# Reordering the second block of a two-block transformer kernel on one core: selection early, attentions mixed with dense products, last lifts by row block

## What is computed

```python
h = rmsnorm(x, norm_mix)
(a_x, a_b, a_c, d_q, d_k, d_v, i_q, i_k, i_w, g_q, g_f, g_i, g_g, m_q, gate_logits) = split_cols(h @ w_in)
y_a = a_b * causal_conv3(a_c * a_x, conv_w)
y_b = dsa_attention(q, k, d_v, iq, ik, iw)      # keys chosen by top-64 of an index score
y_c = hgrn2_chunkwise(hq, hk, hv, log_f)        # then rmsnorm and * silu(g_g)
y_m = softmax(mq @ mk) @ mv                     # 4 heads over 256 memory tokens
merged = sum over n of sigmoid(gate_logits)[n] * (branches[n] @ w_lift[n])
x = x + merged @ w_out
x = x + (silu(gate) * up) @ ffn_w_down          # feed-forward on rmsnorm(x)
```

## Time and profile before

| | us |
|---|---|
| median of 3 runs | 2562.72 (2559.86 to 2564.99) |
| profiled execution | 2557.33 |
| its span, first to last instruction | 2555.6 |
| TensorE matmul busy | 2463.1 (96%) |
| VectorE busy | 1544.4 (60%) |
| ScalarE busy | 1172.0 (46%) |
| GpSimd busy | 101.4 (4%) |
| mean granted TensorE clock | 0.986 |

### The profile page before, as it was taken

How to read it: one execution, slowest core, us unless ns; L and a number is a source line. 1 busy time by engine, 2 the same in 40 slices (tenths; PEclk the granted TensorE clock), 3 DMA queues, 4 the chain that set the end, 5 groups by cost and what they waited for, 6 DMA issues and landing times.

```text
span 2555.6 us, 30973 instructions
## 1 busy us (share of the span) xinstructions
PE 2463.1 (96%) x12352; PEld 2055.9 (80%) x12352; DVE 1544.4 (60%) x2297; ACT 1172.0 (46%) x1621; POOL 101.4 (4%) x132
## 2 busy tenths in 40 slices
PE   7999999999999999999999999998999999998999
PEld 5788888888888778887888888786888887777887
DVE  6855655456546575467655747677555657676544
ACT  4643444444444564436434446344444456344442
POOL 2100000000000010000100000000100000000000
PEclk9999999999999999999999999998999999998999
DMA  7355352342653546533754435342754344343652
GB/s 243 118 202 192 132 198 99 134 163 88 225 198 132 184 146 207 178 147 115 280 197 149 152 128 191 104 165 107 263 198 171 143 164 156 110 159 111 235 180 94
DMA packets 263118, 418.93 MB, mean 164 GB/s; under 512 B 12192, under 2 KB 149408, under 8 KB 262976
## 3 DMA queue, kind: packets, MB, share of 16 engines
q1 hardware_dynamic: 258112, 400.15, 44.4%
q0 software_dynamic: 4864, 16.80, 1.8%
HBM read 415.86 MB, written 1.05 MB: 163 GB/s over the span
## 4 chain that ended last, share of the span: by engine, by line
PE 86%; DVE 9%; ACT 2%; issue 1%; DMA 1%; POOL 1%; SPq 0%; DVEq 0%; ACTq 0%
PE bank_L L1818 36%; PE bank_L L1803 23%; PE bank_S L1987 7%; PE bank_O L1987 7%; PE bank_O L1928 3%; DVE wlo L1148 2%; PE bank_S L1803 1%; PE bank_T L1916 1%; PE bank_T L1970 1%; PE bank_T L1831 1%; PE bank_O L1803 1%; DVE sm L1472 1%; DVE pts L1495 1%; PE bank_S L1889 1%; PE bank_L L1889 1%
## 5 line engine op out<-in xcount | busy, mean ns | idle before, releaser
L1148 DVE TENSOR_TENSOR wlo<-raw,whi 128x2048 fp32r<-128x2048 f32 (+1 forms) x332 | 711.6, 2169 | 293.7 <-ACT whi L897 292.9
L897 ACT ACTIVATE whi<-raw 128x2048 fp32r<-128x2048 f32 (+1 forms) x332 | 592.3, 1817 | 58.2 <-DMA raw<-in_w_in 35.3
L1818 PE MATMUL bank_L<-whi,xt_hi 128*128 128x512 f32 x1376 | 547.5, 398 | 7.7 <-DVE wlo L1148 6.3
L1818 PE MATMUL bank_L<-wlo,xt_hi 128*128 128x512 f32 x1376 | 539.0, 392 | 0.0
L1818 PE MATMUL bank_L<-whi,xt_lo 128*128 128x512 f32 x1376 | 538.3, 391 | 0.0
L1803 PE MATMUL bank_L<-whi,xt_hi 128*128 128x512 f32 (+1 forms) x864 | 338.1, 391 | 5.5 <-DVE wlo L1148 5.5
L1803 PE MATMUL bank_L<-wlo,xt_hi 128*128 128x512 f32 (+1 forms) x864 | 334.8, 387 | 0.0
L1803 PE MATMUL bank_L<-whi,xt_lo 128*128 128x512 f32 (+1 forms) x864 | 334.5, 387 | 0.0
L1040 ACT ACTIVATE tok<-bank_L 128x256 f32<-128x256 f32 x132 | 50.7, 384 | 566.1 <-PE bank_L L1818 566.1
L1818 PEld LDWEIGHTS bank_L<-whi,xt_hi 128*128 128x128 f32 x1376 | 260.3, 189 | 61.2 <-issue 7.1
L1818 PEld LDWEIGHTS bank_L<-wlo,xt_hi 128*128 128x128 f32 x1376 | 259.8, 189 | 55.7
(11 more groups left out here) (285 smaller groups left out, 3280.4 us busy)
## 6 DMA issues: line engine op xcount, KB each, us to landing
raw<-in_w_gate_up SPq DMA_DIRECT2D x176, 512.0 KB, 5.9
raw<-in_w_in SPq DMA_DIRECT2D x72, 1024.0 KB, 6.2
draw<-in_w_down SPq DMA_DIRECT2D x44, 1024.0 KB, 6.3
raw<-in_ffn_w_up SPq DMA_DIRECT2D x88, 512.0 KB, 5.7
raw<-in_b_w_qkv SPq DMA_DIRECT2D x36, 1024.0 KB, 6.9
draw<-in_ffn_w_down SPq DMA_DIRECT2D x22, 1024.0 KB, 6.1
raw<-in_w_lift SPq DMA_DIRECT2D x32, 512.0 KB, 4.5
raw<-in_a_w_qkv SPq DMA_DIRECT2D x12, 1024.0 KB, 8.2
```

The lines of the kernel that those rows point to most:

```text
L897: act.activation(wide(whi, w, nkc, ncols)[:, ks, :], wide(raw, w, nkc, ncols)[:, ks, :], ACT.Copy) \
L1148: dve.tensor_tensor(wide(wlo, w, nkc, ncols)[:, ks, :], wide(raw, w, nkc, ncols)[:, ks, :], wide(whi, w, nkc, ncols)[:, ks, :].bitcast(F32 ...
L1818: mm = pe.matmul(banks[bank][:, :], xx[:, k, t * P:(t + 1) * P], ww[:, k, :], start=(k == 0 and q == 0), stop=(k == KC - 1 and q == 2))
```

## The change

Only the second block's stage list and what serves it are changed.

- `norms` replaces the layer and RMS norms: same arithmetic, row blocks interleaved, one GpSimd round per row block. `rows_of` replaces `split(r)`: row block 0 is turned inside the mem V product (`mid`), row block 1 inside the pair IQ, MQ.
- A stage of kind `fill` is a product that is cut into 16 steps of k (3 matmuls each, 6 of half width if turned) and dealt out over the steps of another stage: gate (3,1) over select, DQ over the memory attention, AC and AB over the DSA attention, gate (2,0) over HGRN (its row block 0 ahead of the states, 1 ahead of the outputs).
- Selection is early. New order: mem K, mem V, IQ and MQ, narrow chunk, gate (3,0), select with gate (3,1), head norm and turn of MQ, memory attention with DQ, lifts 3, gate (1,0), gate (1,1), AX, DSA attention with AC and AB, gate (0,0), conv, lifts 1, GF, GQ, gate (0,1), lifts 0, GI, GG, HGRN with gate (2,0), gate (2,1), lifts 2, w_out. The eight top-k rounds are a stage `topk` in three parts: ahead of gate (1,0), of gate (1,1) and of AX.
- An attention with fill rotates its scores through S0 and S1 alone.
- Conv writes its result in float32 and a stage `conv_end`, behind lifts 1, splits it.
- `lifts`: the last two lifts go row block by row block, with r's row block 0 turned ahead of the last quarter and row block 1 turned inside the first product of w_out.

```diff
+            add("select", iqT=iqT, kkT=kkT, sel=sel, ready=is_turned, fill=[gate_st])
+            q_ok = headnorm(heads_of(tc, 128), 4, 128, gains[:, l, 256:384], is_in[1])
+            turn(tc, q_ok, mqT)
+            add("exp_table")
+            st = linear(lhs, w_cols(C_DQ), NW, "act", dst=tc, after=[])
...
+            o_is = attention(units, 128 ** -0.5, [], (turn_done, n["turn"]), [], fill=[st], ps=ps2)
             ylhs = split(ym, o_is, (yt_hi, yt_lo), nkc=4)
-            lift(3, ylhs, gates(3), first=True)
+            lift(3, ylhs, 0, gate_0, first=True)
+            lift(3, ylhs, 1, gate_1, first=True)
+            add("topk", sel=sel, rounds=(0, 3))
...
+            gate_01 = gate(0, 1, tb)
+            add("decays", l=l, counts=counts)
+            lift(0, ylhs, 0, gate_00)
+            lift(0, ylhs, 1, gate_01)
...
+        def filled(fill, i, steps):
+
+            per, total = T * KC, T * KC * len(fill)
+            a, b = total * i // steps, total * (i + 1) // steps
+            return [(st, max(a - q * per, 0), min(b - q * per, per)) for q, st in enumerate(fill)
+                    if a < (q + 1) * per and b > q * per]
...
+        def split_at(fill, i, steps):
+
+            for q, st in enumerate(fill):
+                for h in range(2):
+                    if i == (2 * q + h) * steps // (2 * len(fill)):
+                        return [st["w"] + 1, (h,)]
+            return None
```

VectorE's part of an attention and of the last lifts, and TensorE's last lines in a step:

```diff
+                    steps = len(U) + 3
+                    for i in range(steps):
                         if i < len(U):
                             maxima(i)
-                        if i >= 2:
+                        if 2 <= i < len(U) + 2:
                             copies(i - 2)
                             reciprocal(i - 2)
+                        if split_at(st["fill"], i, steps):
+                            split_lo(*split_at(st["fill"], i, steps))
...
+                elif st["kind"] == "lifts":
+                    w = st["w"]
+                    split_upto(w + 1)
+                    for half in range(2):
+                        lifted(w + half, 0, half, (SB, OB)[half][0], st["held"][half])
+                    lifted(w, 1, 0, SB[1], st["held"][0])
+                    rows_lo(st["rows"], 0)
+                    lifted(w + 1, 1, 1, OB[1], st["held"][1])
+                    split_upto(w + 2)
...
+                        for late, a, b in filled(st["fill"], i, len(U) + 3):
+                            product(late, a, b)
```

More of the change, by code:

```diff
@@ L250, in renorm @@
             st = add("renorm", norm=norm, dst=dst, alpha=alpha, lhs=lhs, bias=bias, w=n["w"], gbv=n["gb"],
-                     rows=x if norm == "layer" else r)
+                     rows=x if norm == "layer" else r, second=second[0] if lhs else None,
+                     when=[(x_ready, n["xr"] + t + 1) for t in range(T)])
+            second[0] = None
             if lhs:
@@ L594, in lift @@
[L594 to L609, removed]
-            conv_in = (aev, n["aev"])
-            ym = blk(3).rearrange("p (t c) -> p t c", t=T)
+            def gate(branch, half, dst):
+                linear(lhs, w_cols(C_GATE + branch * D + half * NW), NW, "act", dst=dst, func=ACT.Sigmoid,
+                       after=[(dev, n["dev"]), (rope_done, n["rope"])])
+                return (dst, n["aev"])
@@ L686, in build @@
+            headnorm(heads_of(tc, HD), 8, HD, gains[:, l, 0:64], dq_in)
+            q_ok = rope(heads_of(tc, HD), 8, 1, dq_in)
+            turn(tc, q_ok, dqT)
+            add("exp_table")
+            fill = [linear(lhs, w_cols(c0), NW, "act", turned=True, dst=blk(b_).rearrange("p (h s) -> p h s", s=SEQ), after=[])
+                    for b_, c0 in ((1, C_AC), (2, C_AB))]
+            conv_in = (aev, n["aev"])
             units = []
@@ L694, in build @@
                 units.append(dict(rows=rows, dv=HD, sink=None))
-            o_is = attention(units, HD ** -0.5, [(aev, small_ok[1])], (turn_done, n["turn"]), [gate_st], lead=0, in_twos=True)
-            ylhs = split(yb, o_is, (yt_hi, yt_lo), nkc=4)
-            lift(1, ylhs, held_gates)
+            o_is = attention(units, HD ** -0.5, [(aev, small_ok[1])], (turn_done, n["turn"]), [], in_twos=True, fill=fill,
+                             ps=ps2)
+            gate_00 = gate(0, 0, tc)
+            add("conv", l=l, after=conv_in)
@@ L698, in build @@
+            add("lifts", lhs=ylhs, rows=second[0], held=(gate_0, gate_1), w=n["w"])
+            for half in range(2):
+                chunks.append(([(0, cols(w_lift[l, 2], half * NW, (half + 1) * NW))], 4, NW))
+            for t in range(T):
+                for half in range(2):
+                    finishes(n["w"] + half, t, t == T - 1)
+            n["w"] += 2
+            n["dev"] += 4
             load_gains([norm_ffn[l]], [(dev, n["dev"]), (o_done, n["unit"])])
-            lhs = split(r, (dev, n["dev"]), (xt_hi, xt_lo))
@@ L1774, in turn_heads, with product @@
                     held[name] = (turn_done, at["turn"] + t + 1)
[L1776 removed]
+            def product(st, first=0, last=None):
                 at = st["at"]
@@ L2052, in _ @@
                         held[name] = (rel_done, at["rel"] + e + 1)
+                        for late, a, b in filled(st["fill"], e, 4 * T):
+                            product(late, a, b)
                 elif st["kind"] == "hgrn":
```

456 lines of the change are left out of this document (273 added, 183 removed).

## The result

The changed kernel takes **2572.14 us** (median of 7 runs, 2567.3 to 2576.11), the kernel before 2559.86 beside it: ratio 1.0046, 95% interval 1.003 to 1.0062. It is **slower by 12.3 us**, where 20 less was forecast, and lies above the range. A repetition (first experiment) gives 1.0041.

What follows compares the result with a forecast made beforehand. TensorE's dense products were taken to set the pace, with only overhead to win. Terms of -10.9 and -9.4 us in the two layers sum to -20.3: 2542.4 for the median, 2537.0 for the profiled execution; range 2520 to 2566.

Steps and rivals of the forecast that it cites:

- norms: Mem K to third product: rows turned inside products, weight split following them on VectorE; -5.6 / -1.4 us.
- select: Scores interleaved with a gate product: overhead 6.2 us, little dearer than the unstalled second layer; -4.4 / -0.1 us.
- mq behind select: Head norm of mq after select's last accumulation, uncovered: TensorE stands 8.2 us, plus 2 for the clock; +10.2 / +10.2.
- memory attention: Attention over the memory with DQ as fill: 9.1 us of overhead plus 1.2 bare ahead of the lift; -1.2 / -1.2.
- DSA attention: Filled with two turned products: 11.2 us own work plus 4.5 of waits from half-splits of weights; -3.5 / -7.3.
- conv, forget gates: Conv moved under a gate product, its split behind the lifts: new overhead 0 and 0.6 us; -3.8 / -8.8.
- first lifts, branch 0: Decay exponentials delay the second lift's split on ScalarE: wait 3.9 us, GI's split 0.6, clock 1.5; +6.0 / +6.0.
- HGRN: A gate product as fill closes both gaps, leaving 9.0 us; -5.1 / -3.4.
- last lifts, w_out: Lifts by row block, then w_out: TensorE waits 3.8 us for its split, stage 40.3; -4.3 / -4.2.
- Top-k: Eight rounds moved under lifts, gates and AX: 43 us of VectorE work fits 44.3 of products, DQ's turn late; +0.8 / +0.8.
- Rival 4: Slower: lower clock in filled stretches, 192 us in all; slower by over 5 from a 13% share, 2590 at a quarter; chance 0.07.
- Rival 3: DSA attention fill paced by VectorE's and ScalarE's queues, every half-split bare: 33 us instead of 9, 2566; chance 0.12.

Runs made afterwards that it cites:

- e1: Changed kernel with VectorE's head norm of mq issued ahead of select instead of behind it: 2548.79 us, ratio 0.9958.
- e4: Changed kernel with VectorE's head norm and rope of DQ issued ahead of AX instead of behind its split: 2556.24 us, ratio 0.999.
- e7: Changed kernel with mq and DQ norms earlier, w_out's first split between last lifts, decays behind first lifts, third gate's weights split ahead of the logarithms: 2511.31 us.
- e11: e7 with DSA attention half-splits one step later and, second layer, the first lift's split ahead of the second logarithms: 2499.76 us, ratio 0.9784.
- e12: e7 with coarser fill in select (two groups of scores, then 12 matmuls): 2511.5 us.
- e15: e11 with mq's head norm put back behind select: 2522.2 us, ratio 0.9854.
- e8: e7 with select unfilled, gate product (3, 1) as a whole behind the scores: 2517.04 us.
- e14: e11 with the fills of select and of both attentions undone: 2515.17 us, ratio 0.9825.
- e0: The changed kernel repeated unaltered beside the kernel before: 2570.55 us, ratio 1.0041.
- e13: e11 with coarser fill in select (two groups of scores, then 12 matmuls): 2498.41 us, ratio 0.9762, the best version.

## Why the prediction was wrong

Forecast and measured change of each term, first layer / second layer, from the windows above (dense work taken off as the forecast did). The mq row is the wait of 7.8 with the 2.3 and 2.6 that the attention behind it takes over the 20.0 of e1; the memory attention's row is that 20.0 and the 1.1 ahead of its lift:

| term | forecast | measured |
|---|---|---|
| norms | -5.6 / -1.4 | -4.9 / -1.3 |
| select | -4.4 / -0.1 | -2.0 / +2.3 |
| mq behind select | +10.2 / +10.2 | +10.1 / +10.4 |
| memory attention | -1.2 / -1.2 | -1.3 / -1.3 |
| turn of DQ late | +0.8 / +0.8 | +5.3 / +5.2 |
| DSA attention | -3.5 / -7.3 | -1.5 / -6.1 |
| conv, forget gates | -3.8 / -8.8 | -2.6 / -3.1 |
| first lifts, branch 0 | +6.0 / +6.0 | +5.7 / +6.9 |
| HGRN | -5.1 / -3.4 | -4.6 / -2.9 |
| last lifts, w_out | -4.3 / -4.2 | -3.6 / -2.8 |
| sum | -10.9 / -9.4 | +0.6 / +7.3 |

Some 2 us more per layer lie in turns and products outside these windows.

**What held.** The waits that were looked for came as foretold: mq 7.8 (8.2 forecast), lifts 4.0 (3.9), w_out 3.9 (3.8). A bare wait for the first DSA scores came too, at 2.3. All told, the gaps that the forecast named were right to a few tenths. Its sum for the DSA attention's own work comes to 11.0 where it says 11.2, and the queue of *Top-k* to 0.5 where it says 0.8; neither matters.

**The step that failed is *Top-k*:** "VectorE's queue there ... 43 us of work with 1.8 of waits for the first transfer, against 44.3 of products. The turn of DQ is late by 0.8." It summed VectorE's work and one wait. The queue has a second, 3.16 behind ScalarE, and a GpSimd round 1.27 longer than mq's, together 4.4; the turn was late by 5.3 and 5.2. With its clock the late turn is worth 15 us (e4) where 1.6 was forecast: alone enough to turn -20 into about -7 (part of the 15 stands in the table's row for the DSA attention). The rest of the way to +12 is, by the table, in the two steps that follow (6.9 and 4.8 too low in sum), in the DSA attention (3.2), in the last lifts (2.1) and in the 4 us outside the windows, which the forecast put at nothing.

**Next, *Conv and the forget gates*,** second layer: "New overhead 0 and 0.6". VectorE idles 7.4 for the logarithms, and the next weights' split stands behind them:
```profile
2246.78 1.23 DVE L1743 SCALAR_TENSOR_TENSOR arena<-arena 128x1024 f32<-128x1024 f32 x1 [7.39 <-ACT arena L1181]
...
2253.85 4.49 DVE L1234 TENSOR_TENSOR wlo<-raw,whi 128x2048 fp32r<-128x2048 f32 x2
```
TensorE waits 4.5, and the gate product behind begins at the lower clock. It is the same fault, a queue costed as a sum. In e7, with the split ahead of the logarithms, the 4.5 went and 3.25 came back one product further; e11 removed that too.

**Then *Select*:** "Interleaved it can't be dearer than that by much ... overhead 6.2". It was 8.6. Six matmuls take 1.59 instead of 1.36 and each of the first groups of scores 0.64 instead of 0.43, a price per change of kind (e12). Eight times some 0.4 on the 5.2 of the scores themselves (four groups at 0.43, four at 0.87) makes the 8.6.

**The clock** was added behind mq, at the first lifts and in the last stage, 5 per layer, and behind mq the size was right (2 forecast, 2.3 and 2.6 measured). None was added for the gaps that the forecast missed, and the clock was not seen as what the fill is for. Rival 4 had it backwards: filled select was granted 1.00 in both layers, and so was HGRN. The filled attentions read 0.88 to 0.95, so one sign of being wrong, PEclk under 0.9 in a filled stretch, did come (0.89 and 0.88 over the memory); but they stand behind the long waits, and in e11, with the same fill and without those waits, both layers read 1.00. The Trainium skill, TensorE: Matmul & The Clock Gate, A second HAM failure mode: psum-queue depth-cycling, whose rule was weighed there, is not borne out by those rows. The lower level stands behind waits (e15) and in bare thin stages (e8, e14).

Rival 3, fill paced by the two queues, named the right engines but the wrong place: not the half-splits inside the DSA attention (2.3 and 3.1 of wait, 5.4 in both layers, not 33), but what stands ahead of the two attentions and of the lifts. 2572 lies above its 2566 as well, the upper end of the range.

Left open: how much of the clock each wait owns. The single removals gained 23, 12, 15 and 15 where their waits were 15.6, 7.8, 8 and 10.5, but lower stretches also move between stages.

## What to carry to other kernels

When work is dealt out as fill, write down for every engine the order of its queue with the time at which each entry can *start*; a sum of busy times hides an entry that waits for another engine and holds up a head norm that is long ready. Put norms that feed a coming stage ahead of splits that can wait, and order what is behind before adding fill: here four moved pieces of order made a loss of 0.4% a gain of 1.8%, and eight changes a gain of 2.4%. Seven of them without the fill of select and of both attentions already gave 1.75% (e14).

## What the hardware showed that was not expected

- A wait of TensorE of 7.8 cost 10.4 and 11.2: 1.0 more up to the next scores, the rest in the stage behind at PEclk 0.93 and 0.88 (e15). The kernel before itself lost much to the lower level: busy TensorE time 383.3 and 380.0 at 0.95 and 0.96 against 367.5 and 367.1 at 1.00 in e11, for the same products.
- Changing between groups of 64-row scores and dense 512-column matmuls costs about 0.4 per round trip (e12: 4.46 against 4.04 for the same work with one round trip less).
- ScalarE's and VectorE's work hardly changed in any version (VectorE 268 to 271 busy per layer); the time moved by 72 us between e0 and e13 by order, by the coarser fill (some 3), and by what the clock made of it.
